# Who stores the final rows, and in which two steps they are scaled

## The reference, cut to what matters

```python
def rmsnorm(x, g):
    xf = x.astype(jnp.float32)
    y = xf * lax.rsqrt(jnp.mean(xf * xf, axis=-1, keepdims=True) + RMS_EPS)
    return (y * g.astype(jnp.float32)).astype(x.dtype)
...
    up = rmsnorm(x, g_ffn_pre) @ ffn_w_up                # 1024 -> 2 * 2816
    ext = jnp.concatenate([conv_hist, up], axis=1)
    c = ffn_conv_b
    for j in range(CONV_W):
        c = c + ext[:, j: j + T] * ffn_conv_w[j]
    act = jax.nn.gelu(c[..., :D_FF], approximate=True) * c[..., D_FF:]
    x = x + rmsnorm(act @ ffn_w_down, g_ffn_post)        # 2816 -> 1024, then the result y
```

## Time and profile before

| | |
|---|---|
| median of three runs | 1677.47 us (1677.42 to 1682.96) |
| the profiled execution | 1676.98 us |
| its span, first to last instruction | 1675.3 us |
| granted TensorE clock, mean | 0.973 |
| PE busy | 1607.9 us, 96% |
| DVE busy | 731.4 us, 44% |
| ACT busy | 564.0 us, 34% |
| POOL busy | 146.3 us, 9% |

### The profile page before, as it was taken

How to read it: one execution, slowest core, us unless ns; L and a number is a source line. 1 busy time by engine, 2 the same in 40 slices (tenths; PEclk the granted TensorE clock), 3 DMA queues, 4 the chain that set the end, 5 groups by cost and what they waited for, 6 DMA issues and landing times.

```text
span 1675.3 us, 24740 instructions
## 1 busy us (share of the span) xinstructions
PE 1607.9 (96%) x9631; PEld 1510.0 (90%) x9631; DVE 731.4 (44%) x1198; ACT 564.0 (34%) x1061; POOL 146.3 (9%) x193
## 2 busy tenths in 40 slices
PE   6999999999999999979879999999999999999996
PEld 6889999999999999968769999999999997888885
DVE  6474563756231221453444334343434345454533
ACT  7232231333122123224323333333333334343432
POOL 0123242331000000000000000000000000000000
PEclk9999999999899999989979999999999999999998
DMA  7134354341423411350025466545642127565650
GB/s 245 53 117 149 124 193 154 126 125 58 123 81 89 120 51 38 102 176 0 0 94 185 150 198 207 184 156 182 208 134 65 65 74 247 177 210 176 208 163 29
DMA packets 143472, 219.25 MB, mean 131 GB/s; under 512 B 13137, under 2 KB 115969, under 8 KB 142504
## 3 DMA queue, kind: packets, MB, share of 16 engines
q1 hardware_dynamic: 132791, 191.38, 36.0%
q0 software_dynamic: 9648, 26.01, 4.1%
q10 hardware_dynamic: 969, 0.99, 0.2%
HBM read 192.53 MB, written 70.02 MB: 157 GB/s over the span
## 4 chain that ended last, share of the span: by engine, by line
PE 93%; DVE 4%; ACT 1%; issue 1%; ACTq 0%; POOL 0%; POOLq 0%; DVEq 0%
PE PS L977 48%; PE PS L1159 16%; PE PS L873 9%; PE PS L1108 6%; PE PS L858 4%; PE PS L1041 2%; PE PS L930 2%; PE PS L902 1%; PE PS L916 1%; PE PS L840 1%; PE PS L886 1%; DVE hn L1541 1%; DVE sga L1844 0%; DVE merged L1847 0%; DVE wo_lo L1849 0%
## 5 line engine op out<-in xcount | busy, mean ns | idle before, releaser
L977 PE MATMUL PS<-hT_hi,tw_hi 128*128 128x352 f32 x1536 | 343.6, 332 | 1.6 <-issue 1.5
L977 PE MATMUL PS<-hT_hi,tw_lo 128*128 128x352 f32 x1536 | 335.8, 327 | 0.0
L977 PE MATMUL PS<-hT_lo,tw_hi 128*128 128x352 f32 x1536 | 335.2, 327 | 0.0
L1665 DVE TENSOR_TENSOR tw_lo<-tw_stage,tw_hi 128x1024 fp32r<-128x1024 f32 x74 | 88.9, 1203 | 456.5 <-ACT tw_hi L1301 456.2
L977 PEld LDWEIGHTS PS<-hT_hi,tw_lo 128*128 128x128 f32 x1536 | 267.7, 191 | 0.0
L977 PEld LDWEIGHTS PS<-hT_hi,tw_hi 128*128 128x128 f32 x1536 | 265.0, 193 | 2.5 <-issue 1.9
L977 PEld LDWEIGHTS PS<-hT_lo,tw_hi 128*128 128x128 f32 x1536 | 265.4, 191 | 0.0
L1301 ACT ACTIVATE tw_hi<-tw_stage 128x1024 fp32r<-128x1024 f32 x74 | 74.9, 1014 | 258.9 <-PE PS L977 258.4
L1918 DVE TENSOR_TENSOR wd_lo<-wd_stage,wd_hi 128x1024 fp32r<-128x1024 f32 x66 | 80.8, 1225 | 138.2 <-ACT as_hi L1464 136.2
L1941 DVE SCALAR_TENSOR_TENSOR cacc<-cext,cols,cacc 128x1024 f32<-128x1024 f32 x88 | 113.1, 1285 | 56.3 <-ACT cacc L1487 27.8
L1159 PE MATMUL PS<-wd_hi,as_hi 128*128 128x512 f32 x396 | 123.6, 393 | 1.1 <-ACT cnat L1496 1.1
(11 more groups left out here) (234 smaller groups left out, 2286.7 us busy)
## 6 DMA issues: line engine op xcount, KB each, us to landing
wd_stage<-in_ffn_w_down SPq DMA_DIRECT2D x66, 512.0 KB, 3.5
tw_stage<-in_ffn_w_up SPq DMA_DIRECT2D x44, 512.0 KB, 3.9
out_k_s<-in_cache_k_w SPq DMA_DIRECT2D x8, 2044.0 KB
out_v_s<-in_cache_v_w SPq DMA_DIRECT2D x8, 2044.0 KB
qb<-zs SPq DMA_DIRECT2D x24, 512.0 KB, 5.3
acts<-cact POOLq DMA_DIRECT2D x22, 528.0 KB, 8.0
tw_stage<-in_w_in SPq DMA_DIRECT2D x20, 512.0 KB, 5.0
as_stage<-acts SPq DMA_DIRECT2D x44, 192.0 KB, 3.8
```

Of the source, the lines that this page charges most:

```text
L977: last = pe.matmul(PS[:, 3 * s + b, 0:BW], w[s][:, k, :], x[:, k, b * BW:(b + 1) * BW], start=(k == 0 and j == 0), stop=(k == kc - 1 and j ...
L1665: dve.tensor_tensor(tw_lo[s][:, 0:kc, :], tw_stage[s][:, 0:kc, :], tw_hi[s][:, 0:kc, :].bitcast(F32), ALU.subtract).then_inc(tw_lo_done, 1)
```

## The change

The result's stores leave POOL's list and come onto SP's. The tiles 0 to 2 are stored behind the load of chunk 30, the tiles 3 to 5 behind that of chunk 52, the tiles 6 to 8 behind the last load. There are three row buffers in place of two. DVE first multiplies the PSUM tile with the norm weight, as soon as ACT has squared the tile, then takes the reciprocal, and multiplies by it and adds the residual in one instruction.

```diff
-        ytmp = [sb1(f"ytmp{s}", [P, D]) for s in range(2)]
+        ytmp = [sb1(f"ytmp{s}", [P, D]) for s in range(3)]
...
+            def store_y(n):
+                sp.wait_ge(y_ready, n + 1)
+                dst, part = (ys, slice(OWN, P)) if n == 8 else (yp[n * P:n * P + P], slice(0, P))
+                sp.dma_start(dst, ytmp[n % 3][part, :]).then_inc(y_out[n % 3], 16)
             for q in range(NWD, len(DOWN)):
                 load_down(q)
-
-            for s in range(2):
-                sp.wait_ge(y_out[s], 16 * (5 if s == 0 else 4))
+                if q % FC == 8 and q > FC:
+                    for x in range(3):
+                        store_y(3 * (q // FC - 1) + x)
+            for n in range(6, NTILE):
+                store_y(n)
+
+            for s in range(3):
+                sp.wait_ge(y_out[s], 16 * 3)
...
-            for n in range(NTILE):
-                pool.wait_ge(y_ready, n + 1)
-                dst, part = (ys, slice(OWN, P)) if n == 8 else (yp[n * P:n * P + P], slice(0, P))
-                pool.dma_start(dst, ytmp[n % 2][part, :]).then_inc(y_out[n % 2], 16)
...
+                    dve.wait_ge(o_ss, 9 + n + 1)
+                    if G:
+                        dve.wait_ge(y_out[x], 16 * G)
+                    dve.tensor_tensor(ytmp[x][0:rows, :], PS[0:rows, 2 * pair:2 * pair + 2, :].rearrange("p b n -> p (b n)"),
+                                      gfin[0:rows, :], ALU.mult).then_inc(f_free, 1)
                     dve.wait_ge(o_rms, 9 + n + 1)
-                    dve.reciprocal(prstd[:, 1, n:n + 1], prms[:, 1, n:n + 1]).then_inc(f_step, 1)
+                    dve.reciprocal(prstd[0:rows, 1, n:n + 1], prms[0:rows, 1, n:n + 1]).then_inc(f_step, 1)
                     dve.wait_ge(f_step, n + 1)
-                    dve.wait_ge(y_out[n % 2], 16 * (n // 2))
-                    dve.scalar_tensor_tensor(ytmp[n % 2][:, :], PS[:, 2 * pair:2 * pair + 2, :].rearrange("p b n -> p (b n)"),
-                                             prstd[:, 1, n:n + 1], gfin[:, :], ALU.mult, ALU.mult).then_inc(f_free, 1)
                     dve.wait_ge(f_free, n + 1)
-                    dve.tensor_tensor(ytmp[n % 2][:, :], ytmp[n % 2][:, :], xnat[:, n, :], ALU.add).then_inc(y_ready, 1)
+                    dve.scalar_tensor_tensor(ytmp[x][0:rows, :], ytmp[x][0:rows, :], prstd[0:rows, 1, n:n + 1], xnat[0:rows, n, :],
+                                             ALU.mult, ALU.add).then_inc(y_ready, 1)
```

More of the change, by code:

```diff
@@ L479, in build @@
         y_ready = sem("y_ready")
-        y_out = [sem(f"y_out{s}") for s in range(2)]
+        y_out = [sem(f"y_out{s}") for s in range(3)]
         state_out = sem("state_out")
@@ L1972, in _ @@
                     pair = n % 4
+                    rows = P
+                    dve.wait_ge(o_ss, 9 + n + 1)
[3 more added lines that the diff above has]
+                                      gfin[0:rows, :], ALU.mult).then_inc(f_free, 1)
                     dve.wait_ge(o_rms, 9 + n + 1)
-                    dve.reciprocal(prstd[:, 1, n:n + 1], prms[:, 1, n:n + 1]).then_inc(f_step, 1)
+                    dve.reciprocal(prstd[0:rows, 1, n:n + 1], prms[0:rows, 1, n:n + 1]).then_inc(f_step, 1)
                     dve.wait_ge(f_step, n + 1)
-                    dve.wait_ge(y_out[n % 2], 16 * (n // 2))
-                    dve.scalar_tensor_tensor(ytmp[n % 2][:, :], PS[:, 2 * pair:2 * pair + 2, :].rearrange("p b n -> p (b n)"),
-                                             prstd[:, 1, n:n + 1], gfin[:, :], ALU.mult, ALU.mult).then_inc(f_free, 1)
                     dve.wait_ge(f_free, n + 1)
-                    dve.tensor_tensor(ytmp[n % 2][:, :], ytmp[n % 2][:, :], xnat[:, n, :], ALU.add).then_inc(y_ready, 1)
+                    dve.scalar_tensor_tensor(ytmp[x][0:rows, :], ytmp[x][0:rows, :], prstd[0:rows, 1, n:n + 1], xnat[0:rows, n, :],
+                                             ALU.mult, ALU.add).then_inc(y_ready, 1)
 _OUT = [("y_prompt", (1, TP, D)), ("y_sample", (NB, NT, D)), ("pool_p", (1, 1, HIST, PW)), ("pool_s", (1, NB, HIST, PW))]
```

## The result

The changed kernel takes **1669.56 us** (median of nine runs, 1665.6 to 1673.37) against 1678.07 us before (nine runs, 1674.51 to 1682.96): ratio 0.995, 95% interval 0.9935 to 0.9965. Faster, by 8.5 us or 0.5%; whether by a little over or a little under half a per cent, these runs cannot say. Forecast were 1668.7 us and 8.75 us.

The account below looks back on a forecast made before the run. PE's matmuls bound the kernel, so gain could come only after its last one, mostly from POOL's closing drain. 7.75 us drain, 0.65 us DVE and 0.35 us take-up and landing: 1677.47 - 8.75 = 1668.7 us, range 1667.7 to 1671.3.

Parts of the forecast that it names:

- The end was POOL's drain: Program's end: POOL's 10.16 us drain after its last store outlasts SP's by 7.75 us; without POOL's stores that goes.
- What the drain is: Program's end: the last 8 us are POOL closing its list after a store, not the store or its landing.
- rival B: Program's end: POOL's 10.16 us drain begins only when the others arrive, whatever stood before it; 1678.9 us, 5%.
- Rival A: Program's end: any issuer of a late store pays, so SP drains 10.16 us; gain 0.9 us, 1676.6 us, 9%.
- The row work: DVE, last tiles: PSUM multiplication 1.22 us, multiply-and-add 1.28 us; tile 8 ends at 1664.0 against 1664.65, 0.65 us gained.
- The last store: Program's end: SP issues it at 1664.0, landing taken as 2.1 us, with bounds of 1.8 and 3.8 us.
- Stores between loads: SP behind chunk 30: three issues of 0.33 us, 5.2 us transfer; load 31 may be 17 us late; no cost.
- rival C: SP's queue behind chunks 30 and 52: stores delay loads by 27.6 us, PE waits 21 us in all; 1690 us, 3%.
- The sum: Whole gain 8.75 us: 7.75 us POOL's drain, 0.65 us DVE, 0.35 us faster take-up and landing.
- The range: Whole time 1667.7 to 1671.3 us, from the last store's landing and the multiplication, with 0.5 us for the medians.

Follow-up runs that it names:

- stores alone: Kernel before with only its stores moved to SP, two row buffers and old row instructions kept: 1670.45 us against 1679.73 us, ratio 0.9952.
- stores_x8: Changed kernel with 21 more 512 KB stores on SP behind the loads of chunks 30 and 52 each: 1704.42 us, one run.
- after: The changed kernel itself, with the whole change against the kernel before: 1669.56 us against 1678.07 us, ratio 0.995.
- rows_only: Changed kernel with its nine stores back on POOL; three row buffers and new row instructions stay: 1676.72 us, ratio 0.9986 to the kernel before.
- last_on_sp: Changed kernel with the stores of tiles 0 to 7 on POOL and only that of tile 8 on SP: 1673.4 us, one run.

## Why the prediction was right

*The end was POOL's drain.* Right, and this step carries the gain: stores alone 8.6 us, row work alone 0.8 us, both 8.9 us. They overlap by 0.5 us: the wait of 0.33 us for a row buffer is in both, and the rest is within the rounding of the four tails.

*What the drain is.* Here the prediction's account was too narrow. It spoke of POOL closing its list after a store, and rival B of a drain that is paid "whatever stood before it". B was right in that half and wrong in the other: it is paid whatever stood before, but where POOL comes to its end, not where the others arrive. The sum did not depend on it, since the change empties POOL's list from the convolution on. A change that had left POOL a late step, a mere wait even, would have lost 7 of the 9 us again (tails of 13.1 against 6.3 us). Nor is a drain only the wait for an engine's own outstanding work, as the words ahead of the prediction have it. For DVE that fits; before, its drain ends with its last add:

```profile
L96 DVEq DRAIN  x1: 1264/1264/1264, 1663.4 to 1663.4; - x1
```

For POOL it does not: 8.9 us with nothing outstanding.

The Trainium skill's rule that such drains are a constant of about 12 ns ("VectorE: DVE Perf Modes", The DRAIN you can't avoid) fits SP in every kernel here, 7 to 13 ns, and never POOL, 8.9 to 10.4 us; the measurement decides. It does not fit the closing drains of ACT, DVE and PE either (0.32, 1.26 and 4.35 us before). The page speaks of drains from the code that the runtime puts around a kernel; those here stand at line 96, in the kernel's own block, and may not be meant.

*Rival A*, that the cost goes along with the stores, is out: SP drains in 7 ns right behind a store of its own.

*The row work.* The multiplication out of PSUM took 1.22 to 1.23 us (1.22 expected) and multiply-and-add 1.28 us. The last row was expected 3.9 us into the tail and came at 3.76, since the reciprocal starts a little before the multiplication's end.

*The last store.* Landing 2.0 us, 2.1 expected; of the rows it was taken from, the two of the same size with little beside them (2.0 and 2.2 us) were the good guides, not the 3.8 us beside heavy traffic.

*Stores between loads.* No wait, as forecast, though two sizes were off. Among the loads an issue took SP 0.8 us on average (2.46 us for three) in place of 0.33. And three stores were put at 5.2 us of transfer, but each landed late:

```profile
DMA to landing us min/median/max: 2.0/7.2/8.8
```

This row is of line 723 after, all nine stores. The six stores among loads took 6.8 to 8.8 us. The lead of 17 us covers both, and `stores_x8`, with 27.3 us of waiting against 28 forecast, fits a lead of that size. The delay that rival C needed did not come: load 31 went out no later in the stage than before, and no load around the stores took more than 8.2 us to land.

*The sum.* 8.75 us were forecast, the tail gave 8.9 us, the medians 8.5 us, the span of the one profiled execution 7.4 us, as that execution began the stage 1.5 us later.

*The range.* That the median of 1669.56 us lies inside 1667.7 to 1671.3 is in part luck. Six of the nine runs lie outside it, between 1665.6 and 1673.4 us. The 0.5 us that the range had for the medians were too few: the kernel before has a median of 1677.47 us over three runs, 1678.07 over nine with those three among them, and 1679.73 over 18 others. What bears the prediction out is the tail. From PE's end to the last row, the kernels `after`, `rows_only` and `last_on_sp` all take 3.76 us, and their closings differ as worked out for each.

## What to carry to other kernels

Look behind the last landing: when the span goes on after it, read which engine's closing instruction ends last, and give that engine nothing late to do, not even a wait. Before stores are put among loads on one queue, work out how long the reader of the loads can do without them; up to that lead they were free here, and in the one case beyond it nearly every us was paid. A gain of half a per cent is read from a stretch that is counted from one and the same event, since whole times differ by as much from run to run.

## What the runs showed that I had not expected

POOL's drain takes 8.9 us from where POOL comes to it, with nothing issued for 270 us. What POOL does in that time no row shows. No run here shows a program in which POOL never issued a DMA, so whether it is owed to that stays open too.

Runs of one kernel differ by up to 8 us, and the mean granted clock goes with it: after, 1665.6 us at 0.978 and 1673.4 us at 0.972. The lag of the profiled execution is largely such a case. Early in the run, where nothing was changed, PE has just waited 2.1 us for DVE in both kernels and then makes the same matmuls. Busy time by stretch (columns as above) and the matmuls that come next, before and then after:

```profile
126.00:128.00 2.00, 2.00 (x19) 2.00 (x18) 0.27 (x1) 0.00 (x0) 0.00 (x0) 1.00 0.95 336
...
128.16 0.50 PE L902 MATMUL PS<-qkT,qkT 64*128 64x128 f32 x4
```

```profile
126.00:128.00 2.00, 2.00 (x10) 2.00 (x11) 0.99 (x2) 0.00 (x0) 0.00 (x0) 0.50 0.93 279
...
130.36 0.50 PE L908 MATMUL PS<-qkT,qkT 64*128 64x128 f32 x4
```

PE is busy in both, but with a granted clock of 0.50 it gets through 10 of these matmuls in place of 19. PE took up the stretch 0.7 us later than before (125.84 against 125.12) and leaves it 2.2 us later; at the last stage the lag is 1.5 us. So the clock put 1.5 us into it here; the rest, which comes and goes, I did not follow.
